# A two-block transformer kernel: five landing slots for weight slabs in place of six, loops of twenty slabs, gated stages written out

## Chip, cores and metric

The kernel runs on one core of a Trainium2 chip. The metric is the device time of one execution in microseconds (us): the median of the runs of one kernel. All times below are for 256 tokens, fp32 inputs and outputs.

## The reference, cut to what matters

Two blocks of two layers each work on one sequence of 256 tokens of width 1024. Every weight matrix is used once. In the first block the mixers are differential plus block attention (layer 0) and gated linear attention (layer 1), in the second block grouped attention with rotary positions and cross-attention into a memory of 256 rows. The stages that the change touches are the four feed-forward stages and the stream of weights that feeds all stages:

```python
def sqrelu_mlp(x, w1, w2):                       # first block, D_FF = 4096, twice
    return jnp.square(jax.nn.relu(x @ w1)) @ w2

def conv_gated_ffn(h, w_up, conv_w, conv_b, w_down):   # second block, D_FF_2 = 2816, twice
    u = h @ w_up
    up = jnp.pad(u, ((0, 0), (1, 1), (0, 0)))
    u = up[:, :-2] * conv_w[0] + up[:, 1:-1] * conv_w[1] + up[:, 2:] * conv_w[2] + conv_b
    gate, val = u[..., :D_FF_2], u[..., D_FF_2:]
    return (jax.nn.silu(gate) * val) @ w_down

x = layer_norm(DEEPNORM_ALPHA * x + mix, g, b)   # after each mixer of the first block
x = x + memory_cross_attention(...)              # second block, followed by rmsnorm and the FFN
```

## The kernel before

**The stream of weights.** The weights are packed beforehand into 205 slabs of 128 x 2048 fp32 (1 MB each), in the order of their use. A slab goes through four hands. The DMA queue of the sync engine (SP) loads it into a landing slot `raw` (line 374). ScalarE (ACT) copies it, rounded to fp32r, into a slot of `wh` (`split`, line 529). VectorE (DVE) writes the rest, `raw - wh`, as `wl` over the landing slot itself (line 888; `raw` and `wl` are the same memory, line 154); for four slabs GpSimd (POOL) does that (line 414). TensorE (PE) multiplies with both, three products for each pair of tiles: high x high, high x low, low x high. After its last product PE counts `slab_used` up.

**The rings.** `wh` has RING = 4 slots, `raw`/`wl` has LOWS = 6. So the load of slab s waits until slab s-6 is used (line 373), and the copy of slab s waits until slab s-4 is used (line 528) and until its load has landed (line 526). ACT and DVE split a slab LOOKAHEAD = 3 slabs ahead, at fixed places of their programs.

**The stages.** hy_in, hy_out, ffn0, gla, gla_out, ffn1, mem0, qkv, wo, xq0, xo0, conv0, mem1, xq1, xo1, conv1. Five stages are output projections (`project_out`, lines 1495 on): hy_out, gla_out, wo, xo0 and xo1. Each has four slabs. PE works through all four for the first 128 tokens (t = 0), then through all four for the second 128 (t = 1), and counts each slab as used only in the second pass. So ahead of it lie the attention or scan stages in which no slab is freed, and then four slabs are freed one behind the other.

**Behind a projection.** DVE adds the residual and normalises, first t = 0, then t = 1, and its order is written out by hand. In the first block (`ln_mix`): both column halves of t = 0, split of the stage's slab 1 + 3, first half of t = 1, split of slab 2 + 3, second half of t = 1. In the second block (`residual_rms`) it is the same order with other operations. The last of these halves is line 913 (first block) or line 982 (second block). The two splits are those of the next stage's slabs 0 and 1. PE fills its wait for t = 1 with 14 products of zeros (`stay_warm`, line 1468), transposes (line 1461), and then ACT and DVE split the transposed activations (lines 536 and 901) for the next stage.

**The feed-forward stages.** A squared stage has 16 groups of two slabs: `up` (line 1534 to 1539), ReLU on ACT (625), square on DVE (1083), high part on ACT (627), low part on DVE (1085), and `down` (1553 to 1555), which PE does one group late. Groups 1 to 12 run as a hardware loop of TURN = 12 slabs, in two passes; groups 0, 13, 14 and 15 are written out. A gated stage has 11 groups of three slabs; groups 1 to 8 run as a loop of 12 slabs in two passes, 0, 9 and 10 are written out. Inside a loop a wait compares with a register (`at`, line 136 on), and the taps of the convolution are addressed by a register. A loop needs a turn that is a whole number of both rings.

Of the kernel before, what the change touches and what calls it, by code (L numbers as in the profile page):

```python
# [38 lines left out]

SLAB = 2048  # L40
RING = 4
LOWS = 6
LOOKAHEAD = 3
TURN = 12
CH = 512
GLA_COLS = 3088
SQ_GROUPS = D_FF // 256
CV_GROUPS = D_FF2 // 256
# [92 lines left out]
def build(nc, d):  # L141
    st, S = plan()
    out = d["out"]
    with ExitStack() as ctx:
        def sb(name, shape, dt=F32):
            return ctx.enter_context(nc.sbuf_tensor(name, shape, dt))
# [5 lines left out]
        wh = sb("wh", [P, RING, SLAB], F32R)  # L152
        wl = sb("wl", [P, LOWS, SLAB], F32R)
        raw = nc.alloc_sbuf_tensor_at("raw", [P, LOWS, SLAB], F32, offset=nc.sbuf_base - 4 * LOWS * SLAB)
        xh = sb("xh", [P, KT, T], F32R)
# [75 lines left out]
        def pair(s, n):  # L231

            return [v.rearrange("p (k n) -> p k n", n=n) for v in (wh[:, s % RING, :], wl[:, s % LOWS, :])]

# [4 lines left out]

        raw_loaded = [sem(f"raw_loaded{i}") for i in range(LOWS)]  # L240
        wh_ready = sem("wh_ready")
# [128 lines left out]
        def _(sp):  # L370
            def load(s):
                if s >= LOWS:
                    sp.wait_ge(slab_used, s - LOWS + 1)
                sp.dma_start(raw[:, s % LOWS, :], d["w_slabs"][s]).then_inc(raw_loaded[s % LOWS], 16)
# [139 lines left out]
        def _(act):  # L514
# [101 lines left out]
            def ffn(name, base):  # L616
# [4 lines left out]
                def group(g, i=None):  # L621

                    up = s0 + 2 * g - 1 if g else s0
                    act.wait_ge(slab_used, at(i, TURN, up + 1))
                    nc.scalar.activation(r[:, g % 2, :], ps[g % 2][:, :], ACT.Relu).then_inc(bank_free, 1)
# [19 lines left out]
            def conv(name, l, base, cbase):  # L645
                stage = st[name]
                s0 = stage.s0
                cg, cv, sg, h = ar(CV_G, 2, 2, T), ar(CV_V, 2, 2, T), ar(CV_S, 2, CH), ar(CV_H, 2, CH)

                def mid(bank, dst, ft, i):  # L650

                    for a in range(2):
                        f = at(i, 8, ft + a)
                        ins = nc.scalar.activation(dst[:, a, :], bank2(bank)[:, a, :], ACT.Identity,  # L654
                                                   scale=cw[:, l, 1, bass.ds(f, 1)], bias=cw[:, l, 3, bass.ds(f, 1)])
                    ins.then_inc(conv_mid, 1)

                def group(g, i=None):

                    up = s0 + 3 * g - 1 if g else s0  # L660
                    if g:
                        split(up + LOOKAHEAD, i, 12)
                    act.wait_ge(slab_used, at(i, 12, up + 1))
                    mid(2 * (g % 2), cg[:, g % 2], 2 * g, i)
                    split(up + 1 + LOOKAHEAD if g else up + LOOKAHEAD, i, 12)
                    act.wait_ge(bank_free, at(i, 8, stage.f0 + 4 + 2 * g + 1))
                    nc.scalar.activation(sg[:, g % 2, :], cg[:, g % 2].rearrange("p a t -> p (a t)"), ACT.Silu).then_inc(gate_act, 1)
                    act.wait_ge(slab_used, at(i, 12, up + 2))
                    mid(2 * (g % 2) + 1, cv[:, g % 2], FT2 + 2 * g, i)
                    if g < CV_GROUPS - 1:  # L670
                        split(up + 2 + LOOKAHEAD if g else up + 1 + LOOKAHEAD, i, 12)
                    act.wait_ge(hid_sq, at(i, 4, base + g + 1))
                    nc.scalar.activation(hh[:, g % 2, :, :].rearrange("p k t -> p (k t)"), h[:, g % 2, :], ACT.Copy).then_inc(hid_hi, 1)

                group(0)
                n = (CV_GROUPS - 1) // 4
                with act.Fori(0, n) as i:
                    for g in range(1, 5):
                        group(g, i)
                for g in range(1 + 4 * n, CV_GROUPS):  # L680
                    group(g)
                splits(stage, 3 * CV_GROUPS - 2, 3 * CV_GROUPS)

# [8 lines left out]
            g = st["hy_in"]  # L692
# [28 lines left out]
            g = st["gla"]  # L721
# [73 lines left out]
            g = st["mem0"]  # L795
# [16 lines left out]
            g = st["qkv"]  # L812
# [18 lines left out]
            for l in range(2):  # L831
# [4 lines left out]
                g = st[f"xq{l}"]  # L836
# [12 lines left out]
                if l == 0:  # L849

                    g = st["mem1"]
# [20 lines left out]
        def _(dve):  # L872
# [231 lines left out]
            def conv(name, l, base, cbase):  # L1104
                stage = st[name]
                s0 = stage.s0
                cg, cv, sg, h = ar(CV_G, 2, 2, T), ar(CV_V, 2, 2, T), ar(CV_S, 2, CH), ar(CV_H, 2, CH)

                def taps(bank, dst, ft, e, i):

                    dve.wait_ge(conv_mid, at(i, 8, cbase + e + 1))
                    for a in range(2):
                        ins = nc.vector.scalar_tensor_tensor(dst[:, a, 1:T], bank2(bank)[:, a, 0:T - 1], cw[:, l, 0, bass.ds(at(i, 8, ft + a), 1)],  # L1113
                                                             dst[:, a, 1:T], ALU.mult, ALU.add)
                    ins.then_inc(conv_tap, 1)
                    dve.wait_ge(conv_tap, at(i, 8, cbase + e + 1))
                    for a in range(2):
                        ins = nc.vector.scalar_tensor_tensor(dst[:, a, 0:T - 1], bank2(bank)[:, a, 1:T], cw[:, l, 2, bass.ds(at(i, 8, ft + a), 1)],
                                                             dst[:, a, 0:T - 1], ALU.mult, ALU.add)
                    ins.then_inc(bank_free, 1)  # L1120

                def group(g, i=None):
                    up = s0 + 3 * g - 1 if g else s0
                    if g:
                        split(up + LOOKAHEAD, i, 12)
                    taps(2 * (g % 2), cg[:, g % 2], 2 * g, 2 * g, i)
                    split(up + 1 + LOOKAHEAD if g else up + LOOKAHEAD, i, 12)
                    taps(2 * (g % 2) + 1, cv[:, g % 2], FT2 + 2 * g, 2 * g + 1, i)
                    dve.wait_ge(gate_act, at(i, 4, CV_GROUPS * l + g + 1))
                    dve.wait_ge(bank_free, at(i, 8, stage.f0 + 4 + 2 * g + 2))  # L1130
                    nc.vector.tensor_tensor(h[:, g % 2, :], sg[:, g % 2, :], cv[:, g % 2].rearrange("p a t -> p (a t)"), ALU.mult).then_inc(hid_sq, 1)
                    if g < CV_GROUPS - 1:
                        split(up + 2 + LOOKAHEAD if g else up + 1 + LOOKAHEAD, i, 12)
                    dve.wait_ge(hid_hi, at(i, 4, base + g + 1))
                    nc.vector.tensor_tensor(hl[:, g % 2, :, :].rearrange("p k t -> p (k t)"), h[:, g % 2, :],
                                            hh[:, g % 2, :, :].rearrange("p k t -> p (k t)").bitcast(F32), ALU.subtract).then_inc(hid_lo, 1)

                group(0)
                n = (CV_GROUPS - 1) // 4
                with dve.Fori(0, n) as i:  # L1140
                    for g in range(1, 5):
                        group(g, i)
                for g in range(1 + 4 * n, CV_GROUPS):
                    group(g)
                splits(stage, 3 * CV_GROUPS - 2, 3 * CV_GROUPS - 1)

# [4 lines left out]
            g = st["hy_in"]  # L1151
# [88 lines left out]
            g = st["gla"]  # L1240
# [64 lines left out]
            g = st["mem0"]  # L1305
# [10 lines left out]
            g = st["qkv"]  # L1316
# [75 lines left out]
            for l in range(2):  # L1392
# [33 lines left out]
                if l == 0:  # L1426

                    g = st["mem1"]
# [19 lines left out]
        def _(pe):  # L1448
# [159 lines left out]
            def conv(name, base):  # L1608
                stage = st[name]
                s0 = stage.s0  # L1610

                def up(g, i=None):
                    s = s0 + 3 * g - 1 if g else s0
                    for a in range(2):
                        pe.wait_ge(bank_free, at(i, 8, stage.f0 + 2 * g + a + 1))
                        slab_up(s + a, 2 * (g % 2) + a, i=i, step=12, stage=None if g or a else stage)

                def down(g, i=None, last=False):
                    pe.wait_ge(hid_lo, at(i, 4, base + g + 1))
                    slab_down(s0 + 3 * g + 4 if not last else s0 + 3 * g + 2, g % 2, i, 12, last)  # L1620

                open_down()
                up(0)
                n = (CV_GROUPS - 1) // 4
                with pe.Fori(0, n) as i:
                    for g in range(1, 5):
                        up(g, i)
                        down(g - 1, i)
                for g in range(1 + 4 * n, CV_GROUPS):
                    up(g)  # L1630
                    down(g - 1)
                down(CV_GROUPS - 1, last=True)
# [135 lines left out]
            g = st["gla"]  # L1768
# [95 lines left out]
            for l in range(2):  # L1864
                g = st[f"xq{l}"]
# [166 lines left out]
```

## Time and profile before

| | us |
|---|---|
| median of 3 runs (lowest, highest) | 1406.42 (1406.37, 1409.41) |
| the profiled execution itself | 1406.45 |
| its span on the core | 1404.6 |
| PE busy | 1352.6 (96%) |
| DVE busy | 870.1 (62%) |
| ACT busy | 661.7 (47%) |
| 205 weight loads, median from issue to landing | 4.9 |
| mean DMA rate | 166 GB/s |

The profile is of one execution. PE is the busiest engine, so the question to put to every row is whether PE waits for it. Of other engines' idle time only that counts which ends late enough to hold PE. 1.85 us of the profiled execution lie outside of its span.

### The profile page before, as it was taken

The numbers are of one execution on the slowest core, as the hardware profiler recorded it, in microseconds if no ns is written. First come the engines' busy times: TensorE is split into PE (matmuls) and PEld (weight loads), VectorE is DVE, ScalarE is ACT, GpSimd is POOL, SyncE is SP. The second block draws the span as 40 slices with busy tenths as digits, with TensorE's granted clock in tenths as the row PEclk, the third lists the DMA queues.
The fourth block names the chain that finished last, engine by engine and source line by source line (L and its number), as shares of the span: only waits on it lengthen the run. The fifth ranks groups of instructions, "written<-read, shape, count | busy, mean of one in ns | idle before, by whom it ended". The sixth has DMA issues, their size and how long they took to land.

```text
span 1404.6 us, 20256 instructions
## 1 busy us (share of the span) xinstructions
PE 1352.6 (96%) x8456; PEld 1196.1 (85%) x8456; DVE 870.1 (62%) x936; ACT 661.7 (47%) x777; POOL 115.3 (8%) x146
## 2 busy tenths in 40 slices
PE   8978999999999999999997999999999999999997
PEld 6857899997987899999875788899999997899996
DVE  4957655556577755555577564866667544676664
ACT  5443444445644444444553443655555442655552
POOL 2020100000321100001013000100001100000000
PEclk9999999999999999999998999999999999999999
DMA  9531555555442655555650052655556441555550
GB/s 342 192 147 63 209 180 184 196 188 180 150 150 94 221 191 198 180 182 190 213 180 1 9 217 70 230 183 188 194 184 232 144 166 45 184 192 194 180 180 31
DMA packets 34775, 233.56 MB, mean 166 GB/s; under 512 B 3992, under 2 KB 4240, under 8 KB 8464
## 3 DMA queue, kind: packets, MB, share of 16 engines
q1 hardware_dynamic: 30080, 217.07, 43.9%
q0 software_dynamic: 4336, 14.77, 3.1%
q8 instruction: 52, 0.85, 0.2%
q10 hardware_dynamic: 288, 0.72, 0.1%
q14 instruction: 19, 0.16, 0.0%
HBM read 231.49 MB, written 1.05 MB: 166 GB/s over the span
## 4 chain that ended last, share of the span: by engine, by line
PE 88%; DVE 6%; ACT 3%; issue 2%; POOL 1%; DMA 1%; POOLq 0%; SPq 0%; DVEq 0%; ACTq 0%
PE ps L1534 13%; PE ps L1539 13%; PE ps L1535 13%; PE ps L1553 7%; PE ps L1554 7%; PE ps L1555 7%; PE ps L1486 4%; PE ps L1487 4%; PE ps L1488 4%; PE ps L1513 2%; PE ps L1515 2%; PE ps L1514 2%; PE ps L1717 2%; PE ps L1461 1%; PE ps L1691 1%
## 5 line engine op out<-in xcount | busy, mean ns | idle before, releaser
L888 DVE TENSOR_TENSOR wl<-raw,wh 128x2048 fp32r<-128x2048 f32 x201 | 459.5, 2291 | 246.1 <-ACT wh L529 245.9
L529 ACT ACTIVATE wh<-raw 128x2048 fp32r<-128x2048 f32 x205 | 391.5, 1914 | 181.9 <-PE ps L1539 100.9
L1534 PE MATMUL ps<-xh,wh 128*128 128x256 f32 x1544 | 380.0, 284 | 3.0 <-DVE xl L901 2.3
L1535 PE MATMUL ps<-xh,wl 128*128 128x256 f32 x1544 | 378.7, 283 | 0.0
L1534 PEld LDWEIGHTS ps<-xh,wh 128*128 128x128 f32 x1544 | 295.9, 192 | 6.5 <-issue 4.3
L1535 PEld LDWEIGHTS ps<-xh,wl 128*128 128x128 f32 x1544 | 296.1, 192 | 2.1 <-issue 0.2
L1539 PE MATMUL ps<-xl,wh 128*128 128x256 f32 x1544 | 216.7, 283 | 0.0
L1539 PEld LDWEIGHTS ps<-xl,wh 128*128 128x128 f32 x1544 | 199.2, 192 | 0.0
L1553 PE MATMUL ps<-wh,hh 128*128 128x512 f32 x432 | 168.8, 391 | 0.6 <-DVE hl L1085 0.6
L1554 PE MATMUL ps<-wl,hh 128*128 128x512 f32 x432 | 168.7, 390 | 0.0
L1555 PE MATMUL ps<-wh,hl 128*128 128x512 f32 x432 | 168.1, 389 | 0.0
L1486 PE MATMUL ps<-wh,xh 128*128 128x512 f32 x272 | 107.0, 393 | 3.1 <-DVE xl L901 3.1
L1488 PE MATMUL ps<-wh,xl 128*128 128x512 f32 x272 | 105.9, 389 | 0.0
L1487 PE MATMUL ps<-wl,xh 128*128 128x512 f32 x272 | 105.9, 389 | 0.0
L654 ACT ACTIVATE arena<-ps,cw 128x256 f32<-128x256 f32 x88 | 44.9, 561 | 117.6 <-PE ps L1539 117.6
L1555 PEld LDWEIGHTS ps<-wh,hl 128*128 128x128 f32 x432 | 81.1, 188 | 17.3
L1553 PEld LDWEIGHTS ps<-wh,hh 128*128 128x128 f32 x432 | 81.3, 188 | 16.4 <-issue 0.8
L1554 PEld LDWEIGHTS ps<-wl,hh 128*128 128x128 f32 x432 | 81.3, 188 | 14.9
L1113 DVE SCALAR_TENSOR_TENSOR arena<-ps,cw,arena 128x255 f32<-128x255 f32 x88 | 38.5, 478 | 87.6 <-ACT arena L654 87.6
L407 POOL TENSOR_SCALAR rstd<-var 128x1 f32<-128x1 f32 (+2 forms) x32 | 11.1, 347 | 878.9 <-ACT xn L559 404.5
L536 ACT ACTIVATE xh<-ps 128x512 fp32r<-128x512 f32 x64 | 34.1, 596 | 94.0 <-PE ps L1461 94.0
L901 DVE TENSOR_TENSOR xl<-ps,xh 128x512 fp32r<-128x512 f32 x64 | 40.7, 684 | 54.5 <-ACT xh L536 54.5
(212 smaller groups left out, 1503.5 us busy)
## 6 DMA issues: line engine op xcount, KB each, us to landing
raw<-in_w_slabs SPq DMA_DIRECT2D x205, 1024.0 KB, 4.9
qk<-in_mem POOLq DMA_DIRECT2D x2, 1024.0 KB, 5.4
X<-in_x SPq DMA_DIRECT2D x1, 1024.0 KB, 5.7
gains<-in_ln_mix_g POOLq DMA_DIRECT2D x2, 512.0 KB, 5.6
gains<-in_ln_mix_b POOLq DMA_DIRECT2D x2, 512.0 KB, 6.4
gains<-in_ln_ffn_g POOLq DMA_DIRECT2D x2, 512.0 KB, 7.1
gains<-in_ln_ffn_b POOLq DMA_DIRECT2D x2, 512.0 KB, 8.0
gains<-in_mem_norm POOLq DMA_DIRECT2D x2, 512.0 KB, 4.8
```

Source lines behind the costliest of these rows:

```text
L529: nc.scalar.activation(wh[:, s % RING, :], raw[:, s % LOWS, :], ACT.Copy).then_inc(wh_ready, 1)
L654: ins = nc.scalar.activation(dst[:, a, :], bank2(bank)[:, a, :], ACT.Identity, scale=cw[:, l, 1, bass.ds(f, 1)], bias=cw[:, l, 3, bass.ds( ...
L888: nc.vector.tensor_tensor(wl[:, s % LOWS, :], raw[:, s % LOWS, :], wh[:, s % RING, :].bitcast(F32), ALU.subtract)\
L1486: nc.tensor.matmul(o, xh[:, kt, ts], wa[:, k, :], start=(kt == 0), stop=False)
L1487: nc.tensor.matmul(o, xh[:, kt, ts], wb[:, k, :], start=False, stop=False)
L1488: ins = nc.tensor.matmul(o, xl[:, kt, ts], wa[:, k, :], start=False, stop=(kt == KT - 1))
L1534: nc.tensor.matmul(o, wa[:, kt, cs], xh[:, kt, :], start=(kt == 0), stop=False)
L1535: nc.tensor.matmul(o, wb[:, kt, cs], xh[:, kt, :], start=False, stop=False)
L1539: ins = nc.tensor.matmul(o, wa[:, kt, cs], xl[:, kt, :], start=False, stop=(kt == KT - 1))
L1553: nc.tensor.matmul(o, hh[:, par, k, ts], wa[:, k, cs], start=False, stop=False, skip_group_check=True)
L1554: nc.tensor.matmul(o, hh[:, par, k, ts], wb[:, k, cs], start=False, stop=False, skip_group_check=True)
L1555: ins = nc.tensor.matmul(o, hl[:, par, k, ts], wa[:, k, cs], start=False, stop=last and k == 1, skip_group_check=True)
```

## The change

There are five slots for landing and low parts in place of six (8 KB of each partition are free again), and five semaphores for landings. The load of slab s now waits for slab s-5. RING and LOOKAHEAD stay. Since the turn of a loop has to be a whole number of 4 and of 5 slots, the squared stages turn by twenty slabs (ten groups): with 16 groups that makes one pass (groups 1 to 10), and groups 11 to 15 are written out. The gated stages have no such turn and are written out on ACT, DVE and PE.

```diff
@@ -39,9 +39,9 @@
 SLAB = 2048
 RING = 4
-LOWS = 6
+LOWS = 5
 LOOKAHEAD = 3
-TURN = 12
+TURN = 20
@@ -672,12 +672,7 @@
-                group(0)
-                n = (CV_GROUPS - 1) // 4
-                with act.Fori(0, n) as i:
-                    for g in range(1, 5):
-                        group(g, i)
-                for g in range(1 + 4 * n, CV_GROUPS):
+                for g in range(CV_GROUPS):
                     group(g)
@@ -1135,12 +1130,7 @@
-                group(0)
-                n = (CV_GROUPS - 1) // 4
-                with dve.Fori(0, n) as i:
-                    for g in range(1, 5):
-                        group(g, i)
-                for g in range(1 + 4 * n, CV_GROUPS):
+                for g in range(CV_GROUPS):
                     group(g)
@@ -1621,12 +1611,7 @@
                 up(0)
-                n = (CV_GROUPS - 1) // 4
-                with pe.Fori(0, n) as i:
-                    for g in range(1, 5):
-                        up(g, i)
-                        down(g - 1, i)
-                for g in range(1 + 4 * n, CV_GROUPS):
+                for g in range(1, CV_GROUPS):
                     up(g)
                     down(g - 1)
```

## Rows read from the trace of the kernel before

**Rows 1.** The page: an engine's busy us and instructions; the chain by engine.
```profile
PE 1352.6 (96%) x8456; PEld 1196.1 (85%) x8456; DVE 870.1 (62%) x936; ACT 661.7 (47%) x777; POOL 115.3 (8%) x146
...
PE 88%; DVE 6%; ACT 3%; issue 2%; POOL 1%; DMA 1%; POOLq 0%; SPq 0%; DVEq 0%; ACTq 0%
```

**Rows 2.** Windows (stretch, us, busy by engine, clock, DMA): ffn0 twice, then conv0.
```profile
core 0: us, PE busy (x) PEld busy (x) DVE busy (x) ACT busy (x) POOL busy (x), PEclk, DMA share, GB/s
204.81:227.25 22.44, 22.44 (x146) 20.53 (x145) 11.75 (x8) 9.81 (x8) 0.00 (x0) 1.00 0.55 188
288.82:311.26 22.44, 22.44 (x146) 20.52 (x146) 11.76 (x8) 9.80 (x9) 0.00 (x0) 1.00 0.55 188
946.86:980.82 33.96, 33.96 (x241) 32.04 (x241) 22.96 (x26) 17.67 (x18) 0.00 (x0) 1.00 0.53 186
```

**Rows 3.** One line's view: DVE's split, line 888, who waited for it, whole run.
```profile
  PEld ps L1486: 2.8, 1
```

**Rows 4.** ffn0, 160 to 320 us: weight loads' landing, then timeline of a group.
```profile
DMA to landing us min/median/max: 4.7/4.8/5.9
...
182.41 1.92 ACT L529 ACTIVATE wh<-raw 128x2048 fp32r<-128x2048 f32 x1 [3.84 <-PE ps L1539]
...
187.95 0.69 DVE L1085 TENSOR_TENSOR hl<-arena,hh 128x512 fp32r<-128x512 f32 x1 [0.70 <-ACT hh L627]
...
193.43 0.40 PE L1553 MATMUL ps<-wh,hh 128*128 128x512 f32 x1
```

**Rows 5.** Around xq0's start, 803 to 822 us: loads, splits, the last residual half.
```profile
805.40 0.33 SPq L374 DMA_DIRECT2D raw<-in_w_slabs  x1
...
DMA to landing us min/median/max: 4.8/4.8/4.8
...
805.46 1.92 ACT L529 ACTIVATE wh<-raw 128x2048 fp32r<-128x2048 f32 x1 [0.90 <-PE ps L1515]
...
807.41 2.29 DVE L888 TENSOR_TENSOR wl<-raw,wh 128x2048 fp32r<-128x2048 f32 x1 [4.04 <-ACT wh L529]
...
811.41 2.28 DVE L888 TENSOR_TENSOR wl<-raw,wh 128x2048 fp32r<-128x2048 f32 x1
813.62 0.68 DVE L982 TENSOR_TENSOR X<-ps,X 128x512 f32<-128x512 f32 x1
```

**Rows 6.** Around ffn0's start, 130 to 149 us: the same, and PE's second transpose.
```profile
133.34 0.33 SPq L374 DMA_DIRECT2D raw<-in_w_slabs  x1
...
DMA to landing us min/median/max: 5.4/5.4/5.4
...
138.97 2.27 DVE L888 TENSOR_TENSOR wl<-raw,wh 128x2048 fp32r<-128x2048 f32 x1
141.52 0.69 DVE L913 SCALAR_TENSOR_TENSOR X<-X,ps 128x512 f32<-128x512 f32 x1 [0.28 <-PE ps L1515]
...
146.47 1.09 PE L1461 MATMUL ps<-con,X 128*128 128x128 f32 x8 [1.10 <-DVE X L931]
```

**Rows 7.** Around ffn1's start, 450 to 472 us: load, landing, the last half.
```profile
451.98 0.33 SPq L374 DMA_DIRECT2D raw<-in_w_slabs  x1
...
DMA to landing us min/median/max: 5.1/5.1/5.1
...
460.15 0.69 DVE L913 SCALAR_TENSOR_TENSOR X<-X,ps 128x512 f32<-128x512 f32 x1 [0.23 <-PE ps L1515]
```

**Rows 8.** Around conv0's start, 874 to 890 us: load and last half (landing: rows 5's).
```profile
875.48 0.33 SPq L374 DMA_DIRECT2D raw<-in_w_slabs  x1
...
883.70 0.68 DVE L982 TENSOR_TENSOR X<-ps,X 128x512 f32<-128x512 f32 x1
```

**Rows 9.** Around conv1's start, 1194 to 1210 us: load, landing, last half.
```profile
1195.69 0.33 SPq L374 DMA_DIRECT2D raw<-in_w_slabs  x1
...
DMA to landing us min/median/max: 4.9/4.9/4.9
...
1203.91 0.68 DVE L982 TENSOR_TENSOR X<-ps,X 128x512 f32<-128x512 f32 x1
```

**Rows 10.** Windows again (columns of rows 2): two stretches in which PE stood idle.
```profile
11.55:13.89 2.34, 0.00 (x0) 0.00 (x0) 2.34 (x3) 2.34 (x4) 2.18 (x4) 1.00 1.00 417
...
88.50:93.50 5.00, 0.01 (x1) 0.00 (x0) 4.55 (x7) 1.51 (x8) 3.12 (x1) 0.76 0.00 0
```

**Rows 11.** One line's view: the load issued at 496.1 us, issue to landing.
```profile
DMA to landing us min/median/max: 6.8/6.8/6.8
```

## The prediction, made before the changed kernel ran

> **What bounds the kernel now.** I read the page first: PE is busy in 96% of the span and the chain of work that ended last is 88% PE [rows 1]. So time is lost only where PE waits. The windows view shows that in the feed-forward stages it does not wait at all: 22.44 us busy of 22.44 us [rows 2]. DVE's and ACT's shares (62% and 47%) are no bound. Then I asked the view of one line whom DVE's split of a slab ever held: PE once, for 2.8 us, in the whole run [rows 3]. The stream of weights is therefore hidden today, and the question is whether it still is with one slot less. What remains of the chain, 6% DVE and 3% ACT, lies between stages, where a residual and a norm must be finished before PE can go on: there I looked at the timeline.
>
> **Part 1, the loops.** Removed are one back edge of each squared stage, and in each gated stage the back edge and the loop itself: six tests of a loop in all (2 passes to 1, twice; 2 passes to none, twice), with waits against registers. The stretch 204.81 to 227.25 us of ffn0 holds four slabs and the loop's back edge (group 6 to 7, at 221.5); 288.82 to 311.26 holds four slabs written out. Both take 22.44 us with PE busy throughout. Six slabs of conv0 across its back edge are 33.96 us of 33.96 [rows 2]. A loop costs PE nothing that could be given back, so I take 0. The bounds: 0.01 us, a window's rounding, for each of some six edges below zero, and for written-out code the same above, since the written-out window is as full. On ACT and DVE the freed register work is cover, not path: they are busy 9.8 and 11.8 us of 22.44.
>
> A rule of the Trainium skill weighs here: Advanced Engine Details and Errata, section Control Flow Timing, gives about 108 ns for a compare-and-branch. By it six branches fewer would be an estimated 0.6 us; the trace shows none of this on PE, since the window with an edge is not longer, so the row decides.
>
> **Part 2, five slots in steady running.** The load of slab s is issued when slab s-5 is used, not s-6: one slab later. In ffn0 a slab takes PE 22.44 / 4 = 5.61 us [rows 2]. ACT's copy of slab s starts as slab s-4 is used, so the landed slab used to wait for ACT (5.61 x 2 less a load); now a load has 5.61 us. Loads there take 4.7 to 5.9, median 4.8 [rows 4], which leaves 0.8 us at the median and a copy that is 0.3 us late at the worst. Behind the copy on ACT stands the ReLU and with it the hidden values: DVE finishes `hl` at 187.95 + 0.69 = 188.64 and PE first uses it at 193.43 [rows 4], 4.8 us later. A late copy is hidden by those 4.8 us. Cost 0; without that cover it would be at most 0.3 us in a few groups. The gated stages have three slabs to a group and the same load. I take 0. At the start six loads queued behind one another become five: DMA is full either way. Cost 0.
>
> **Part 3, five slots behind an output projection.** Here the extra slot did work. During attention nothing is used, so all slots are full. Before, the slots held the projection's four slabs and the next stage's 0 and 1. Now they hold only slab 0; slab 1 can be issued only when the projection's first slab is used, which is the moment at which its slab 2 was issued before. DVE has the split of slab 1 in its program ahead of the last residual half of t = 1 (line 913 or 982), and behind that half stand norm, transposes and the start of the next stage, that is PE. The chain goes through there: PE transposes t = 1 at 146.47 after idling 1.10 us for DVE [rows 6]. So each us by which this split comes late is a us of the run. Step by step, with xq0 [rows 5]: the load issued at 805.40 lands after 4.8. ACT is idle then and copies at once (its copy is now due at 808.2 without a landing to wait for). From start of copy to start of DVE's split are 807.41 - 805.46 = 1.95 us. From start of this split to start of the next DVE instruction are 813.62 - 811.41 = 2.21. Together 4.16 us behind the landing.
>
> - xq0: 805.40 + 4.8 + 4.16 = 814.36; the half began at 813.62 [rows 5]: +0.74
> - ffn0: 133.34 + 5.4 + 4.16 = 142.90 against 141.52 [rows 6]: +1.38
> - ffn1: 451.98 + 5.1 + 4.16 = 461.24 against 460.15 [rows 7]: +1.09
> - conv0: 875.48 + 4.8 + 4.16 = 884.44 against 883.70 [rows 5, 8]: +0.74
> - conv1: 1195.69 + 4.9 + 4.16 = 1204.75 against 1203.91 [rows 9]: +0.84
>
> Sum +4.8 us. In ffn0 and ffn1 this is after the 0.28 and 0.23 us that DVE idled there for PE, which the times of start contain [rows 6, 7]. The landings are those of loads issued at the very same moments with the same loads behind them, one slab number higher; that is why I take them and not the run's median. Nothing absorbs the shift later: ACT's copies of slabs 2 and 3 come after the transposed activations and their loads have landed long before. The bounds: with every load at 4.7, the least of ffn0 [rows 4], the five terms are +0.68, +0.69, +0.64, +0.64, +0.64 = +3.3; with every load at 5.9, the most there, each is 1.2 higher: +9.3.
>
> Here the skill's DMA: Bandwidth & Descriptors, section Bandwidth, gives 6.15 us for a transfer of 1 MB. By it the five terms would be about 2.1 us each, an estimated +10.5 us, and a load in steady running would outlast a slab. The trace shows 4.8 for the same size [rows 4, 5], so the measured numbers make the sum.
>
> The profiled execution has 1406.45 us with a span of 1404.6; its median is 1406.42, the same. 1406.45 + 4.8 = 1411.2.
>
> **The rivals.**
> *A, absorbed.* The wait of DVE is there, but the last half is not what PE waits for, or the loads come quicker with fewer in flight. For: DVE idled 0.28 us before the half in ffn0 [rows 6], so there was once some room. Against: PE idles for exactly this chain [rows 6]. Time: 1406.5 to 1408.
>
> *B, contention.* One slot less means that loads sit closer to their use, and a load that meets another transfer is long: 5.9 in ffn0 [rows 4], 6.8 once in ffn1 [rows 11]. Written-out code is also fetched by DMA, so more such meetings. Two of the five at 5.9 instead of 4.8 add 2.2 us: 1413.4. All five at 5.9 make 1406.45 + 9.3 = 1415.8. In steady running it would decide only from a load of 5.61 + 4.8 = 10.4 us on.
>
> *C, the clock.* In ffn0 PE's idle time before the second transpose grows from 1.10 to 2.5 us. PE's granted clock stayed at 1.00 (2.4 GHz) through 2.34 us of idle at the start, and fell (mean 0.76 of the stretch, the lower level is 1.2 GHz) in an idle stretch of 5.00 us [rows 10]. 2.5 is near the first. If it fell and one slab's products (5.6 us by part 2) ran at the lower level, half the speed, before it rose again, that would cost 5.6 us more or less: with half a slab to a whole one, 1414.0 to 1416.8.
>
> *D, faster.* The loops' edges cost PE something that windows of full busy time don't show, since ends of matmuls are modelled. Its place is the six edges. It would have to be worth more than 4.8 us, 0.8 us for each edge, to bring the time below that of before; with 1 us each, and the transitions as forecast, the time is 1405.2; with the transitions absorbed too, 1400.5. Against it: two windows of four slabs, one with an edge, agree to 0.01 us [rows 2].
>
> *E, the change doesn't do what it says.* One pass of a loop is still a loop, so part of the registers' work stays; the price is 0 by part 1, so this is no case with a time of its own.
>
> **How the numbers follow.** Chances: forecast 0.72, A 0.10, B 0.10, C 0.05, D 0.03. About 0.3% (4.2 us) is what a measurement of this kernel can tell from no change. The forecast's own range is 1409.8 (all loads at 4.7) to 1412.5 (one or two of five meet another transfer). It lies close to the border at 1410.6: of its 0.72 I give 0.58 to slower and 0.14 to the same. Slower: 0.58 + 0.10 + 0.05 = 0.73. Same: 0.14 + 0.10 = 0.24. Faster: 0.03. For the range, A and D below and the worst of B above are left out, with half of A's chance above 1408: 1408.5 to 1415.0.
>
> **What would show it.** Right: at the five starts DVE's split of the next stage's slab 1 is released by ACT, and ACT's copy by the landing of a load (before, ACT waited for landings only at the very start); the last half begins some 0.7 to 1.4 us later relative to PE's last product; the windows of ffn0 and conv0 keep 22.44 and 33.96 us; ACT's copies in steady running still start at the release by PE. Wrong: a PE wait on line 888 in a feed-forward stage (part 2), a shorter window there (part 1), a granted clock below 1.00 near 146 us (C), or a shift at the starts that does not reach PE (A).

## The result, and the profile after

| | before | changed | difference |
|---|---|---|---|
| median of 10 runs each, us | 1408.30 | 1412.15 | +3.85 |
| lowest, highest, us | 1406.21, 1409.67 | 1410.37, 1416.03 | |
| ratio with 95% interval | | 1.0038 [1.0028, 1.0047] | |
| profiled execution, span, us | 1404.6 | 1408.5 | +3.9 |

A second series of both kernels on one chip (e11 below) gave a ratio of 1.0025 [1.0016, 1.0034]. Before's own executions spread over 3.5 us, the changed kernel's over 5.7: four of its ten took over 1414 us. So it matters what is compared. The medians differ by 3.85 us (a ratio of 1.0027, just below the table's interval), the means by 4.9. Below, "+3.9" is the difference of the two profiled spans; it is 1.0028 as a ratio.

The page of the changed kernel (busy time by engine; the chain by engine; the queue that fetches instructions):

```profile
PE 1351.4 (96%) x8446; PEld 1195.9 (85%) x8456; DVE 871.8 (62%) x936; ACT 661.3 (47%) x777; POOL 115.1 (8%) x146
...
q8 instruction: 67, 1.10, 0.3%
...
PE 86%; DVE 6%; ACT 3%; DMA 2%; issue 1%; POOL 1%; POOLq 0%; SPq 0%; DVEq 0%; ACTq 0%
```

The line numbers are lower than before's from the gated stage of ACT on: 888 is now 883, 913 is 908, 982 is 977, and PE's are lower by 10 to 15. Only DVE is busy longer, by 1.7 us [rows 1], and not on the path: its instructions take what they took (the split 2.293 us in place of 2.291), and the windows of conv0 below stay full of PE's work. What is new is in the chain: DMA has 2% of it, where it had 1%. So a load now ends a wait on the path. The view of ACT's copy (line 529) lists what it waited for:

```profile
  PE ps L1529: 101.0, 27
  PE ps L1478: 33.8, 12
  DMA raw<-in_w_slabs: 31.4, 10
```

ACT waited ten times for a landing, five times more than before. Two of the five starts, by the timelines of SP, ACT and DVE with the landing of the load; first ffn0, which answers rows 6, then xq0, which answers rows 5:

```profile
133.69 0.33 SPq L374 DMA_DIRECT2D raw<-in_w_slabs  x1
...
DMA to landing us min/median/max: 5.1/5.1/5.1
...
138.86 1.92 ACT L529 ACTIVATE wh<-raw 128x2048 fp32r<-128x2048 f32 x1 [3.18 <-DMA raw<-in_w_slabs]
...
140.81 2.29 DVE L883 TENSOR_TENSOR wl<-raw,wh 128x2048 fp32r<-128x2048 f32 x1 [1.41 <-ACT wh L529]
143.01 0.68 DVE L908 SCALAR_TENSOR_TENSOR X<-X,ps 128x512 f32<-128x512 f32 x1
...
147.96 1.09 PE L1451 MATMUL ps<-con,X 128*128 128x128 f32 x8 [2.24 <-DVE X L926]
```
```profile
807.19 0.33 SPq L374 DMA_DIRECT2D raw<-in_w_slabs  x1
...
DMA to landing us min/median/max: 4.8/4.8/4.8
...
811.97 1.92 ACT L529 ACTIVATE wh<-raw 128x2048 fp32r<-128x2048 f32 x1 [2.80 <-DMA raw<-in_w_slabs]
...
813.92 2.29 DVE L883 TENSOR_TENSOR wl<-raw,wh 128x2048 fp32r<-128x2048 f32 x1 [0.63 <-ACT wh L529]
816.13 0.68 DVE L977 TENSOR_TENSOR X<-ps,X 128x512 f32<-128x512 f32 x1
```

Read from the top: the landing releases ACT, ACT releases DVE, the last residual half stands behind DVE's split, and PE idles 2.24 us in place of 1.10 ahead of its second transpose. In both kernels a load is issued when the projection's first slab has been used (that of the next stage's slab 2 before, of its slab 1 now). So the distance from that issue to the last half measures the step, whatever happened earlier in either execution: in ffn0 141.52 - 133.34 = 8.18 before [rows 6] and 143.01 - 133.69 = 9.32 now, +1.14. In xq0 8.22 before [rows 5] and 8.94 now, +0.72. The other three by the same timelines (issue, then last half: ffn1, conv0, conv1):

```profile
453.47 0.33 SPq L374 DMA_DIRECT2D raw<-in_w_slabs  x1
...
462.38 0.68 DVE L908 SCALAR_TENSOR_TENSOR X<-X,ps 128x512 f32<-128x512 f32 x1
...
877.99 0.33 SPq L374 DMA_DIRECT2D raw<-in_w_slabs  x1
...
886.90 0.68 DVE L977 TENSOR_TENSOR X<-ps,X 128x512 f32<-128x512 f32 x1
...
1198.87 0.33 SPq L374 DMA_DIRECT2D raw<-in_w_slabs  x1
...
1207.76 0.68 DVE L977 TENSOR_TENSOR X<-ps,X 128x512 f32<-128x512 f32 x1
```

They are 8.91, 8.91 and 8.89 against 8.17, 8.22 and 8.22 [rows 7 to 9]: +0.74, +0.69, +0.67. The five make +3.96 us, as much as the span's +3.9. That it is just as much is partly chance. The starts of DVE's 936 instructions, compared one by one, show three other places, which nearly cancel: the changed run begins 0.2 us earlier, loses 0.5 us between 97 and 105 us and wins 0.4 us around 757 us. At the last two PE comes back from the lower granted clock in both executions, but not at the same moment (over 97 to 100 us the clock was 0.84 before and 0.62 now).

The windows of ffn0 and conv0, taken as much later as their stages start now, answer rows 2:

```profile
206.31:228.75 22.44, 22.44 (x145) 20.52 (x145) 11.76 (x8) 9.81 (x8) 0.00 (x0) 1.00 0.52 188
...
950.06:984.02 33.96, 33.96 (x241) 32.04 (x241) 23.16 (x26) 17.66 (x18) 0.00 (x0) 1.00 0.52 186
```

In steady running ACT's copy is still released by PE and not by a landing (timeline of ACT in ffn0, against rows 4), and who waited for DVE's split (against rows 3) is one wait, at a line that is in no feed-forward stage:

```profile
183.97 1.92 ACT L529 ACTIVATE wh<-raw 128x2048 fp32r<-128x2048 f32 x1 [3.84 <-PE ps L1529]
...
  PEld ps L1476: 2.0, 1
```

### The profile page after: what moved, and what is told of

It reads as the page before. It is cut to its first block, busy times and chain, and to the rows that moved or that the text cites. A ratio compares the mean times of both kernels' runs of the same rounds, so it can differ in the third digit from the quotient of the medians.

```text
span 1408.5 us, 19592 instructions
## 1 busy us (share of the span) xinstructions
PE 1351.4 (96%) x8446; PEld 1195.9 (85%) x8456; DVE 871.8 (62%) x936; ACT 661.3 (47%) x777; POOL 115.1 (8%) x146
## 4 chain that ended last, share of the span: by engine, by line
PE 86%; DVE 6%; ACT 3%; DMA 2%; issue 1%; POOL 1%; POOLq 0%; SPq 0%; DVEq 0%; ACTq 0%
PE ps L1524 13%; PE ps L1529 13%; PE ps L1525 13%; PE ps L1543 7%; PE ps L1544 7%; PE ps L1545 7%; PE ps L1476 4%; PE ps L1478 4%; PE ps L1477 4%; DMA raw<-in_w_slabs 2%; PE ps L1702 2%; PE ps L1503 2%; PE ps L1505 2%; PE ps L1504 2%; DVE wl L883 1%
## 5 line engine op out<-in xcount | busy, mean ns | idle before, releaser
L1544 PEld LDWEIGHTS ps<-wl,hh 128*128 128x128 f32 x432 | 81.3, 188 | 14.9
```

The lines of the kernel that those rows point to most:

```text
L1544: nc.tensor.matmul(o, hh[:, par, k, ts], wb[:, k, cs], start=False, stop=False, skip_group_check=True)
```

## The experiments

Theory T: five loads, and through them the place of DVE's split ahead of the last half, make the whole difference. Rivals: steady running with one slab less of lead costs (R1); written-out code costs or gains (R2); the granted clock falls in the longer idle time (C). The numbers 17, 66, 116, 124 and 173 are the slabs 1 of ffn0, ffn1, xq0, conv0 and conv1.

**e1, the loops alone.** Against the changed kernel:
```diff
-LOWS = 5
+LOWS = 6
-TURN = 20
+TURN = 24
```


> Six slots as before, but the gated stages written out and the squared stages in one pass of twelve groups (turn of 24 slabs). Theory (the added 3.9 us are DVE's waits for a landing at the five starts behind an output projection): no change, within 0.3 us of before in the profiled span, every feed-forward stage as long as before. Rival (written-out code costs, by its fetching or by a fuller instruction stream): +2 to +4 us, spread over ffn0, ffn1, conv0 and conv1. Rival (a loop's edge costs PE something that full windows hide): 1 us or more faster.

Measured: ratio 1.0000 [0.9991, 1.0009]. The span was 1405.9, 1.3 us longer than before's. One place in gla, where nothing was changed, costs 1.6 us; the start and the two returns of the clock named above give 0.2 us back in all. PE's windows view shows 14 us around the place in gla, and the 3.4 us in it in which the granted clock was at its lower level (1.2 GHz):

```profile
341.00:355.00 14.00, 14.00 (x79) 10.70 (x78) 4.95 (x4) 9.49 (x12) 0.00 (x0) 0.88 0.37 137
...
348.10:351.50 3.40, 3.40 (x13) 2.59 (x12) 0.69 (x1) 3.37 (x4) 0.00 (x0) 0.50 0.18 77
```

Before's clock there was 1.00. Slab by slab the four feed-forward stages took what they took before, to 0.05 us, but for the first `down` of ffn1, which waits 0.06 us less. R2 falls in both directions.

**e2, five slots with DVE's split moved.** Against the changed kernel, DVE's program:
```diff
                 splits(stage, 1, 2)
                 ln_part(0, 1, w)
-                splits(stage, 2, 3)
                 ln_part(1, 1, w)
...
             prep("ffn0")
-            splits(st["hy_out"], 3, 4)
+            splits(st["hy_out"], 2, 4)
```
and the same in `residual_rms` and behind the other four projections.

> The changed kernel, but DVE's split of the next stage's slab 1 stands behind the transposed activations (with the split of slab 2) and no longer ahead of the last residual half. Theory: the five steps of +1.15, +0.72, +0.71, +0.69 and +0.68 us vanish, the time is that of before within 0.5 us, although slab 1's load still lands as late as in the changed kernel; PE needs that slab only some 12 us after its split now. DVE has 2.3 us more to do at the next stage's start, which slabs 2 and 3 have 5 us and more to spare for. Rivals (steady running with five slots costs; written-out code costs): the 3.9 us stay.

Measured: ratio 1.0007 [0.9998, 1.0016], span 1406.7. ACT and DVE at the start of ffn0 (timeline):

```profile
139.01 1.92 ACT L529 ACTIVATE wh<-raw 128x2048 fp32r<-128x2048 f32 x1 [3.33 <-DMA raw<-in_w_slabs]
...
141.88 0.69 DVE L908 SCALAR_TENSOR_TENSOR X<-X,ps 128x512 f32<-128x512 f32 x1 [2.46 <-PE ps L1503]
...
149.36 6.68 DVE L883 TENSOR_TENSOR wl<-raw,wh 128x2048 fp32r<-128x2048 f32 x3
```

ACT still waits for the landing, but DVE's half is released by PE again, and all five steps are gone. Of the 2.1 us that the span is over before's, 1.6 are a fall of the clock in gla as in e1. One thing I had not allowed for makes 0.8: in ffn1 the first `down` waits that much longer than before, 1.36 us in all for the hidden values' low part, since DVE's extra split there pushes the norm of the memory and the first group (timeline of PE):

```profile
481.84 0.50 PE L1541 MATMUL ps<-wh,hh 128*128 128x512 f32 x1 [1.36 <-DVE hl L1078]
```

**e3, five late loads in the kernel before.**
```diff
-                    sp.wait_ge(slab_used, s - LOWS + 1)
+                    sp.wait_ge(slab_used, s - (5 if s in (17, 66, 116, 124, 173) else LOWS) + 1)
```


> The kernel before, with its six slots and its loops; only five of the 205 loads are held back by one slab, those of slabs 17, 66, 116, 124 and 173 (slab 1 of ffn0, ffn1, xq0, conv0 and conv1). Theory: these five alone give the whole of it, +3.9 us (3.3 to 4.8, by how long the five loads take: a step is issue + load + 4.16 us less the old start of the last half). Rivals (steady running, code): 0.

Measured: ratio 1.0037 [1.0023, 1.0051], in six slots and with the loops: the whole effect. The last halves come 1.24, 0.91, 0.68, 0.66 and 0.96 us later than before, +4.45; these loads took 5.2, 4.9, 4.7, 4.7 and 5.0 us. The span was 1411.1, +6.5. The remaining 2 us lie in three places: 0.4 in the first 130 us, 0.6 around 757 us, and 0.8 at the start of ffn1, where the granted clock was down (window):

```profile
467.90:471.30 3.40, 3.40 (x14) 2.42 (x14) 2.34 (x4) 2.35 (x3) 1.14 (x2) 0.51 0.58 148
```

The first slab there ends 1.65 us late beyond the step. But in the kernel before PE waits 0.59 us for the hidden values at the first `down` of ffn1 (timeline of PE), and after the fall it does not; from the second group on 0.8 us are left.

**e4, the complement: all loads late but these five.**
```diff
-                    sp.wait_ge(slab_used, s - LOWS + 1)
+                    sp.wait_ge(slab_used, s - (LOWS if s in (17, 66, 116, 124, 173) else 5) + 1)
```


> The complement: the kernel before with six slots and its loops, every load held back by one slab as with five slots, but for the same five, which are issued as before. Theory: no change, within 0.3 us of before. Rival (with one slab less of lead the loads in steady running are late for ACT and PE sees it): +3.9 us or a good part of it.

Measured: ratio 0.9995 [0.9986, 1.0004], span 1404.9. No step anywhere above 0.1 us but the 0.2 at the very start. R1 falls. e3 and e4 together are the changed kernel's loads in before's code, but for that of slab 5, which is still issued at the very start here. The lowest ratio of all versions is this one, and its interval takes in no change.

**e8, the same five loads later by one slab more.** As e3, with 4 in place of 5.

> As e3_five_loads_late, but the same five loads are held back by two slabs: each is issued when the projection's second slab is used, 2.72 us later than in e3. Theory (each us by which the landing is later is a us of the run): steps of 3.4 to 4.0 us in place of 0.7 to 1.2 at the five starts, 3.9 + 5 x 2.7 = +17.5 us in all without the clock. PE then idles some 5 us at the starts of ffn0 and ffn1 and some 4 us at the others. If the clock rival is real, PE's granted clock falls there, as it did in a stretch with 5.00 us of idle, and each fall costs about 1.7 us more: up to +26 us. If DVE's order had room of its own, the steps would be smaller than 2.7 above those of e3.

Measured: ratio 1.0227 [1.0209, 1.0244], span 1436.6, +32.0. DVE at the start of ffn0 (timeline):

```profile
144.84 2.29 DVE L888 TENSOR_TENSOR wl<-raw,wh 128x2048 fp32r<-128x2048 f32 x1 [3.89 <-ACT wh L529]
147.05 0.68 DVE L913 SCALAR_TENSOR_TENSOR X<-X,ps 128x512 f32<-128x512 f32 x1
```

The last halves begin 3.68, 3.64, 3.70, 3.77 and 4.20 us after PE's last product in place of 0.04 to 0.09: +18.7 us in all, with 17.5 expected. T holds in its slope. The clock fell at all five starts; windows over each fall:

```profile
151.10:157.90 6.80, 5.90 (x24) 4.90 (x25) 4.89 (x6) 4.50 (x4) 3.69 (x6) 0.50 0.62 203
478.70:482.10 3.40, 3.40 (x14) 2.42 (x14) 2.36 (x4) 2.31 (x3) 1.15 (x2) 0.51 0.68 187
837.10:840.50 3.40, 3.24 (x17) 2.87 (x16) 2.11 (x4) 3.38 (x4) 0.14 (x1) 0.51 0.51 161
912.20:915.60 3.40, 3.40 (x15) 2.44 (x14) 2.19 (x4) 3.40 (x4) 0.00 (x1) 0.50 0.50 165
1236.50:1243.30 6.80, 6.09 (x25) 5.09 (x26) 4.90 (x6) 2.99 (x3) 0.00 (x0) 0.50 0.13 55
```

Taken at the end of the next stage's first slab, the five steps are 28.8 us: 10.1 more than the halves explain, 2.0 for each fall, where I had expected 1.7. They are not alike: where the clock was down for 6.8 us (ffn0 and conv1) the start lost 2.8 us beyond its step, where it was down for 3.4 us 0.8 to 1.6 (0.8 in ffn1, where the first `down` takes half of 1.65 back as in e3). The other 3.2 are falls at 14.5 us and in gla, where nothing was changed; what ffn1 takes back is lost again at the very start and around 757 us.

**e5, every load late by two slabs.** As in e3's line, `s - 4 + 1` for every slab from slab 4 on.

> Six slots and loops as before, but every load is held back by two slabs, as four slots would. Steady running: ACT's copy starts at the landing, 4.8 us after the use of slab s-4, and no longer at that use. The cover of the squared stages is 4.8 us, that of the gated ones 10 us by the same reading of the trace. Theory: PE starts to wait in ffn0 and ffn1, by no more than 0.1 us at a median load and by the excess of each long one, in all 1 to 4 us for each of the two; not at all in conv0 and conv1; and 4.8 us at each of the five starts, since slab 0 of the next stage is late there too: +24. Sum +26 to +32 us, and more where the clock falls. If the cover is less than I read, ffn0 and ffn1 get some us per group longer: over +40 us.

Measured: ratio 1.0470 [1.0447, 1.0494] over two runs, span 1469.5, +64.9: far above what I expected. In the squared stages it went as read. The first row is the window of four slabs of ffn0; the second is from the view of the first product of `down`, and counts its waits for hidden values of squared stages over the whole run:

```profile
184.75:207.63 22.88, 22.69 (x146) 20.57 (x146) 11.76 (x8) 9.60 (x9) 0.00 (x0) 1.00 0.54 184
...
  DVE hl L1085: 7.3, 12
```

22.88 against 22.44 is 0.2 us for a group, and 14 groups of ffn0 came 3.0 us later, those of ffn1 2.7; the last `down` of each waits 1.0 and 1.2 us more. So the cover of 4.8 us was rightly read: a load that is 4.8 us late just shows. The five starts, up to the first groups behind them, lost 12.3, 6.6, 4.8, 9.2 and 6.9 us (DVE's starts against before's), some 40 us in place of 24. What I had left out altogether is that ACT's copy of a slab also stands ahead of work of the attention stages. In the stretch of xo0 (858 to 915 us) ACT waited for landings (waits view):

```profile
ACT wh L529 <- DMA raw<-in_w_slabs: 15.2, 4, 4.2
```

and the stage lost 6.3 us; from mem1 to xo1 it was another 12. The clock was down ten times between the start of ffn0 and the end of conv1, where it was down twice in the kernel before. How much of all this is the clock and how much the waits I did not take apart.

**e6, the split moved in the kernel before.** The edit of e2, with six slots and loops.

> The kernel before with six slots and its loops, and DVE's split of the next stage's slab 1 moved behind the transposed activations, as in e2. Theory: the last residual half began 0.04 us after PE's last product in ffn0 and ffn1 and 0.1 us after it in the others, so there is next to nothing to win: 0.0 to -0.3 us. If DVE's work ahead of the half had been holding PE in the kernel before as well, it would be -1 us or more.

Measured: ratio 1.0010 [0.9999, 1.0021], span 1404.8. The halves begin 0.04 us after PE's last product at all five, 0.05 earlier in three of them, and ffn1's first `down` loses 0.83. Nothing is won. Four of its eleven executions took over 1411 us (up to 1413.16), none of before's over 1409.71, though PE does not idle longer ahead of the second transposes; so such times are no sign of that idle time alone.

**e7, the idle time filled.** In the changed kernel 22 and 21 products of zeros in place of 14 ahead of the second transpose of ffn0 and ffn1.

> The changed kernel with 8 and 7 more products of zeros ahead of the second transpose at the starts of ffn0 and ffn1, which fill 1.7 and 1.5 us of the 2.24 and 1.82 us that PE idles there. They don't lengthen the path. If the longer idle time is what makes the granted clock fall at these starts in some executions (e3's did at 467.9 us and lost 1.8 us by it), the highest times (over 1414 us) become rare and the median is lower by up to 1 us, the lowest stays at +3.9 over before's lowest. If the clock falls elsewhere, median and highest stay as in the changed kernel.

Measured: ratio 1.0024 [1.0015, 1.0032], median 1411.40, one of 12 runs over 1414. The direction is as C expects, but the interval overlaps both series of the changed kernel. Its profile has no fall at either start, and one at 14.9 us, where nothing was changed, for 1.6 us. Inconclusive.

**e9, more idle time without lateness.** In the kernel before:
```diff
-            prep(X, x_ready, x_at("mix0"), warm=14)
+            prep(X, x_ready, x_at("mix0"), warm=9)
```
and the same for mix1.

> The kernel before with 9 products of zeros in place of 14 ahead of the second transpose at the starts of ffn0 and ffn1: PE idles 2.2 us there, as in the changed kernel, in place of 1.1, and no step of the path is later. Theory without the clock: no change. Clock rival (an idle time of 2.2 us is now and then enough for the granted clock to fall): the lowest time stays at before's 1406.3, while some executions are 1.7 to 3 us above before's highest of 1409.7, and the median is up to 1 us higher.

Measured: ratio 1.0010 [1.0001, 1.0020], median 1409.75 against 1407.98 (1.8 us where I expected up to 1), highest 1412.77 against 1410.10. Its profile caught a fall at both starts, with all steps of the path up to them in their old places. PE's timeline of the second transpose of ffn0, then the windows of the two falls:

```profile
148.24 1.97 PE L1461 MATMUL ps<-con,X 128*128 128x128 f32 x8 [2.18 <-DVE X L931]
...
148.20:151.60 3.40, 3.36 (x13) 2.47 (x13) 2.57 (x4) 1.95 (x3) 2.82 (x6) 0.50 0.53 119
469.10:472.50 3.40, 3.40 (x15) 2.42 (x13) 1.99 (x4) 2.97 (x4) 0.85 (x2) 0.50 0.67 171
```

The transposes take 1.97 us in place of 1.09 [rows 6], and the first slab of each of the two stages ends 1.65 us late. In ffn0 these stay lost, in ffn1 0.8 us of them, as in e3. The rest of the span's +5.1 us is a fall at 15.1 us (1.6), where nothing was changed, and the two returns of the clock (0.2 and 0.8). So a fall comes with 2.2 us of idle time, in some executions. The edit also leaves out five products of zeros ahead of it; which of the two the clock answers to is not told apart.

**e10, e2 with 18 products of zeros** in place of 14 at the same places.

> e2 (five slots, the split moved) with 18 products of zeros in place of 14 at the same two places, which fill 0.9 of the 1.1 us that PE idles there. Theory: as e2 or up to 0.5 us better in the median, with fewer times over 1410; with the clock rival wrong: as e2 in median and spread.

Measured: ratio 1.0008 [0.9997, 1.0018], median 1408.87, highest 1412.65: as e2, no better spread. The gain of filling 0.9 us could not be shown.

**e11, the changed kernel again.**

> The changed kernel once more, beside the other two on the same chip. Theory: the lowest time 3.9 to 4.2 us over before's lowest; the five steps in its profile are each the load's time less 3.96 us, within 0.05 us; some executions over 1414 us.

Measured: ratio 1.0025 [1.0016, 1.0034]; median 1412.02, lowest 1409.81, highest 1413.41. The lowest is 3.6 us over before's, a little less than I expected, and none was over 1414. The last halves begin 1.16, 0.98, 0.75, 0.80 and 0.85 us after PE's last product with loads of 5.12, 4.93, 4.70, 4.75 and 4.79 us: each is the load less 3.96 us, to 0.02. This execution's profile has a fall at the start of ffn1, as e3's had: the first slab ends 1.65 us late beyond the step, and 0.8 us stay lost.

## Why the prediction was right, point by point

**The time: closer than its working.** The forecast was 1411.2 us and the median 1412.15, 0.95 over it. The forecast starts from an execution of 1406.45 us, which is near the lowest of the kernel before; its median over ten is 1408.30, 1.85 us more. The added term, +4.8, was 0.95 us more than the medians' +3.85. The two errors have opposite signs and partly cancel, which is luck. The call for "slower" was as narrow as the prediction said: the interval leaves no change out, but +3.85 lies below the 4.2 us that it took as its border.

**The loops (part 1) at 0: right.** e1 shows it by itself, to the 1.3 us of its interval and closer in its stages' lengths, and the windows with and without an edge were a good reading. The 15 further fetches of code (67 packets against 52 before) show nowhere.

**Steady running (part 2) at 0: right.** e4 holds 194 loads back and loses nothing. e5 shows where the cover of 4.8 us ends, at a load 4.8 us late, as the row of `hl` said.

**The starts behind the projections (part 3): the mechanism was right in place, number and form, the size was 0.8 us too large.** Forecast +1.38, +1.09, +0.74, +0.74, +0.84, measured +1.14, +0.74, +0.72, +0.69, +0.67. The mis-sized term is the load. I took the times of the loads issued at the same moments before (5.4, 5.1, 4.8, 4.8, 4.9), on the ground that the same loads stand behind them. They took 5.1, 4.7, 4.8, 4.7, 4.7, and in e3 and e11 yet other times: between the profiles of the changed kernel, e3, e7 and e11 one and the same load varies by up to 0.3 us. The hand-over behind the landing, 4.16 in the forecast, was 4.18 us each time and is not the error. Whether chance is all of it stays open. The five loads together took 24.6 to 25.0 us in the profiles in which they are issued for slab 2 (before, e1, e6, e9), and 24.1 to 24.6 in those in which they are issued for slab 1 (the changed kernel, e2, e3, e7, e10, e11). So they may be a little quicker there; and before's profile, at 25.0, was the slowest of the ten. The low end of the prediction's bounds (4.7 everywhere) gave +3.3, and the sum fell between.

**Rival A** falls by e3 and e8, in which each us of lateness reaches PE, and by e2: take the split from its place and the 3.9 us go. **Rival B** did not occur in the changed kernel: no load at the five starts took more than 5.1 us. **Rival C** was too readily put at 0.05. Its condition is real: the clock fell at four of the eight starts of ffn0 and ffn1 with 1.8 to 2.3 us of idle time (the changed kernel, e3, e9, e11), and at none of fourteen with 1.1 us or less (before, e1, e2, e4, e6, e7, e10). In the first profile of the changed kernel it stayed at 1.00 at both starts. By e9 such a fall costs 1.65 us in ffn0 and 0.8 in ffn1, less than the 2.8 to 5.6 of the prediction, because only part of a slab's products runs in it; 2.8 came only in e8. It adds to the forecast and does not replace it. Its share in the changed kernel's times was not measured: the medians of the two series differ by 3.85 and 4.0 us, hardly more than the five steps, so it may show in the high times (four over 1414 us) and not in the median. **Rival D** falls by e1. As to **rival E**, e1 keeps one-pass loops too and takes before's time, so the registers' work that stays costs nothing that can be measured.

What stays open: how much of the distance between the two series' ratios (1.0038 and 1.0025) is the clock; e7 and e10 did not tell. No version was faster than the kernel before by more than its interval. e2 gives the 8 KB of each partition back at a cost that the interval does not tell from none (-0.02% to +0.16%).

## What to carry to other kernels

A ring's last slot is not priced by steady running, where a late load has other work to hide behind (4.8 us of it in ffn0), but by the places where the ring has stood full and empties at once: count, for each, which slab is now first to be issued there, and follow it through every hand in the order written into the program. There a helper step (here the split of a slab that PE needs 12 us later) can stand ahead of a step that PE needs now. In this kernel moving it makes up for the lost slot (e2), and with six slots it wins nothing (e6). And where PE waits on such a chain, the price of each further us of waiting was here that us plus the risk that the clock falls (e8).

## What the runs showed of the hardware

- The granted clock of PE fell to 0.5 (1.2 GHz) after idle times of 2.0 to 2.2 us between short pieces of work (e3, e9, e11), in some executions and not in others: the changed kernel idled 2.24 us in its first profile at ffn0 and 1.82 at ffn1 and kept 1.00, and e3 kept it through 2.33 us at ffn0. At 13.9 us the kernel before idled 2.38 us and kept it (2.34 of these are in rows 10); with 2.39 to 2.41 us at the same place e7, e8 and e9 had a fall. With 4.0 to 4.7 us of idle (e8) it fell five times out of five.
- A fall that kept the clock down for 3.4 us cost 0.8 to 1.7 us (0.8 where PE had a later wait to absorb part of it, in ffn1), one of 6.8 us 2.8 us (e8, ffn0 and conv1).
- The clock also fell in gla around 348 us, in a stretch in which PE was busy throughout (14.00 us of 14.00 in e1), and cost 1.6 us. It did so in e1, e2 and e10 (at 356 us in e8), and not in before, with the same instructions.
- In all profiles the clock is down for a while around 750 us (last from 746.5 to 756.7 us in the kernel before), where PE stands idle for several us. The moment at which it came back moved the rest of the run by -0.7 (e7) to +0.8 us (e9, e10) against before. A difference of two single profiles below 1 us is therefore to be read place by place.
- From a load's landing through ACT's copy and DVE's split to DVE's next instruction it is 4.18 us, to 0.02, at all five starts of the changed kernel, e3, e7, e8 and e11; the load of 1 MB itself took 4.7 to 5.4 us there.
